# Second block's mixer: row sums from a 65th column of the values that holds 1.0, and distance bias with row maximum as one VectorE operation per map

## The reference, cut to what matters

```
proj = n @ w_in                      # split: c_q c_kv k_r | dq dk dv | mq mk mv
# MLA: 6 heads, causal softmax(q k / sqrt(96)) @ v
# diff: 6 heads with two maps each (width 32), values of width 64
s = q @ k * scale - slope[h] * |pos_q - pos_k|      ; causal mask
p = softmax(s1) - lam * softmax(s2);  o = p @ v
# MoBA: 4 heads of width 64, the same distance bias, one block of 256 keys
s = q @ k * scale - slope[h] * |pos_q - pos_k|      ; causal mask
o = softmax(s) @ v
out = concat(o_mla, rmsnorm(o_diff), o_moba) @ w_out
```

## Time and profile before

| | us |
|---|---|
| time, median of 3 runs (lowest to highest) | 2405.36 (2402.16 to 2407.83) |
| the profiled execution's own time | 2401.76 |
| its span | 2400.0 |
| PE busy in the span | 2357.4 |
| DVE busy | 1726.6 |
| ACT busy | 1446.9 |
| mixer attention, layer 1 of the second stack | from 1575.5 to 1635.4 |
| mixer attention, layer 2 of the second stack | from 2009.3 to 2069.2 |

### The profile page before, as it was taken

How to read it: one execution, slowest core, us unless ns; L and a number is a source line. 1 busy time by engine, 2 the same in 40 slices (tenths; PEclk the granted TensorE clock), 3 DMA queues, 4 the chain that set the end, 5 groups by cost and what they waited for, 6 DMA issues and landing times.

```text
span 2400.0 us, 32057 instructions
## 1 busy us (share of the span) xinstructions
PE 2357.4 (98%) x12122; PEld 1937.0 (81%) x12122; DVE 1726.6 (72%) x2111; ACT 1446.9 (60%) x1761; POOL 69.7 (3%) x79
## 2 busy tenths in 40 slices
PE   9999999999999999999999999999999999999998
PEld 8688888678888888888888888888888888887887
DVE  8664446769898988888989898766465565755555
ACT  6544444657777777777777777564544446554443
POOL 1000000001000000000000000001000000000000
PEclk9999999999999999999999999999999999999999
DMA  7545554429999999999999999516435542452651
GB/s 264 163 158 193 185 186 157 145 82 340 368 345 372 344 377 345 374 339 375 348 369 346 369 350 366 192 54 227 159 124 192 177 145 83 175 187 95 196 190 44
DMA packets 249706, 569.99 MB, mean 237 GB/s; under 512 B 9665, under 2 KB 20353, under 8 KB 249601
## 3 DMA queue, kind: packets, MB, share of 16 engines
q1 hardware_dynamic: 249456, 568.30, 67.1%
q10 hardware_dynamic: 144, 0.26, 0.0%
HBM read 562.82 MB, written 1.05 MB: 235 GB/s over the span
## 4 chain that ended last, share of the span: by engine, by line
PE 92%; DVE 5%; ACT 2%; issue 1%; POOL 0%; POOLq 0%; ACTq 0%; DVEq 0%
PE PS L911 26%; PE PS L913 26%; PE PS L912 26%; PE PS L1064 2%; PE PS L1119 1%; PE PS L1534 1%; PE PS L1076 1%; PE PS L1363 1%; PE PS L1183 1%; PE PS L983 1%; ACT SM L1806 1%; DVE Wl L2216 1%; PE PS L1008 1%; PE PS L1102 1%; PE PS L1324 1%
## 5 line engine op out<-in xcount | busy, mean ns | idle before, releaser
L2645 DVE TENSOR_TENSOR Wl<-ring,Wh 128x2048 fp32r<-128x2048 f32 x334 | 761.6, 2297 | 101.0 <-ACT Wh L1952 101.0
L1952 ACT ACTIVATE Wh<-ring 128x2048 fp32r<-128x2048 f32 x334 | 639.8, 1918 | 127.7 <-PE PS L913 127.7
L2216 DVE TENSOR_TENSOR Wl<-ring,Wh 128x2048 fp32r<-128x2048 f32 (+2 forms) x192 | 431.0, 2251 | 276.6 <-ACT Wh L1713 276.1
L1713 ACT ACTIVATE Wh<-ring 128x2048 fp32r<-128x2048 f32 (+2 forms) x192 | 361.6, 1890 | 235.2 <-PE PS L913 234.2
L911 PE MATMUL PS<-Wh,HTh 128*128 128x512 f32 (+3 forms) x1184 | 464.2, 392 | 4.7 <-DVE Wl L2216 2.4
L913 PE MATMUL PS<-Wh,HTl 128*128 128x512 f32 (+3 forms) x1184 | 456.4, 386 | 0.0
L912 PE MATMUL PS<-Wl,HTh 128*128 128x512 f32 (+3 forms) x1184 | 455.4, 385 | 0.0
L911 PE MATMUL PS<-Wh,xgh 128*128 128x512 f32 x896 | 354.3, 395 | 1.8 <-DVE Wl L2645 1.2
L913 PE MATMUL PS<-Wh,xgl 128*128 128x512 f32 x896 | 349.5, 390 | 0.0
L912 PE MATMUL PS<-Wl,xgh 128*128 128x512 f32 x896 | 348.9, 389 | 0.0
L911 PEld LDWEIGHTS PS<-Wh,HTh 128*128 128x128 f32 x1184 | 222.8, 188 | 50.4 <-issue 4.3
(11 more groups left out here) (349 smaller groups left out, 2422.4 us busy)
## 6 DMA issues: line engine op xcount, KB each, us to landing
ring<-in_moe_w_gate SPq DMA_DIRECT2D x112, 1024.0 KB, 6.9
ring<-in_moe_w_up SPq DMA_DIRECT2D x112, 1024.0 KB, 7.0
ring<-in_moe_w_down SPq DMA_DIRECT2D x112, 1024.0 KB, 6.8
ring<-in_mlp_w SPq DMA_DIRECT2D x64, 1024.0 KB, 5.2
ring<-in_w_in SPq DMA_DIRECT2D x27, 1024.0 KB, 5.3
ring<-in_w_out SPq DMA_DIRECT2D x16, 1024.0 KB, 7.1
ring<-in_cross_wkv SPq DMA_DIRECT2D x16, 1024.0 KB, 12.4
ring<-in_ffn_w_gate SPq DMA_DIRECT2D x14, 1024.0 KB, 5.1
```

The costliest lines, as they stand in the source:

```text
L1713: act.activation(Wh[:, i % SPLITS, 0:n], ring[:, r % RING, 0:n], ACT.Copy).then_inc(w_hi, 1)
L1952: act.activation(Wh[:, (base + i) % SPLITS, :], ring[:, (raw + i) % RING, :], ACT.Copy).then_inc(e_hi, 1)
L2216: dve.tensor_tensor(Wl[:, i % SPLITS, 0:n], ring[:, r % RING, 0:n], Wh[:, i % SPLITS, 0:n].bitcast(F32), ALU.subtract).then_inc(w_lo, 1)
L2645: dve.tensor_tensor(Wl[:, (base + i) % SPLITS, :], ring[:, (raw + i) % RING, :], Wh[:, (base + i) % SPLITS, :].bitcast(F32), ALU.subtract) ...
```

## The change

The values of the three kinds of heads are laid out 65 wide, with the last column set to 1.0 by six `memset`s on DVE at the start of each mixer. The matmul of `values` then gives the row sum of the exponentials as its 65th column, and `end` takes the reciprocal from PSUM. `exps` of these units has no `accum_out`. The bias `dist * s + raw` with its maximum is one `tensor_tensor_reduce` per map that computes (raw + dist) * s and the maximum; for this the queries of the differential and MoBA heads are multiplied with 1/s as they are copied out of PSUM. The columns 1/s are built by POOL at the start, and each copy of two slots with such a factor is now two instructions. Evictions of blocks that hold values are two instructions as well, one of them into the wider layout.

```diff
+                gains = (unsloped(0), unsloped(2, 64)) if slot == 0 else (None, None)
...
+            for k, slopes_ in enumerate(UNSLOPE):
+                pool.memset(unslope[:, k:k + 1], float(np.float32(1.0 / slopes_[0]))).then_inc(pool_seq, 1)
+                n += 1
+            pool.wait_ge(pool_seq, n)
+            for k, slopes_ in enumerate(UNSLOPE):
+                if len(slopes_) > 1:
+                    pool.memset(unslope[64:P, k:k + 1], float(np.float32(1.0 / slopes_[1]))).then_inc(pool_seq, 1)
...
-                            mm = pe.matmul(PS[:, o_bank(un, u), m * dv:(m + 1) * dv],
+                            mm = pe.matmul(PS[:, o_bank(un, u), m * wide:(m + 1) * wide],
...
+                    elif isinstance(gain, list):
+                        for m, g in enumerate(gain):
+                            ins = act.activation(dst[:, m, :], src[:, m, :], ACT.Copy, scale=g)
+                        ins.then_inc(turn_out, 1)
...
-                    if u >= 4:
+                    if u >= 4 and not un["summed"]:
                         act.wait_ge(o_out, u - 3)
                     for m in range(len(un["scores"])):
                         row = SM[:, u % 2, m, 0:un["kl"]]
+                        if un["summed"]:
+                            ins = act.activation(row, row, ACT.Exp, bias=nb[:, u % 2, m:m + 1], scale=un["scale"])
+                            continue
...
+                        src = PS[:, 4 + (c.lin - 1) % 4, :]
+                        if k == 2:
+                            spread_heads(DVS[:, t, 0:4, 0:64], src[:, 256:512], rs_t)
+                            act.activation(proj[:, t, c0:c0 + 256], src[:, 0:256], ACT.Copy, scale=rs_t).then_inc(lin_out, 1)
+                        else:
+                            spread_heads(DVS[:, t, 4:6, 0:64], src[:, 0:128], rs_t)
+                            act.activation(proj[:, t, MQ_AT:MQ_AT + 384], src[:, 128:512], ACT.Copy,
+                                           scale=rs_t).then_inc(lin_out, 1)
...
-                    act.activation(proj[:, t, c0:c0 + n], PS[:, 6, 0:n], ACT.Copy,
-                                   scale=row_rs[:, 0, t:t + 1]).then_inc(lin_out, 1)
+                    rs_t = row_rs[:, 0, t:t + 1]
+                    act.activation(proj[:, t, MK_AT + 128:MK_AT + 256], PS[:, 6, 0:128], ACT.Copy, scale=rs_t)
+                    spread_heads(MVS[:, t, :, 0:64], PS[:, 6, 128:384], rs_t).then_inc(lin_out, 1)
...
-                            ins = dve.scalar_tensor_tensor(out=tile[:, m, :], in0=un["bias"][1], scalar=s,
-                                                           in1=raw[:, m, :], op0=ALU.mult, op1=ALU.add)
+                            ins = dve.tensor_tensor_reduce(tile[:, m, :], raw[:, m, :], un["bias"][1], s, -3e38,
+                                                           ALU.add, ALU.max, mx[:, u % 2, m:m + 1])
                         seq(ins)
-                    if un["bias"] is None or un["bias"][0] != "shared":
+                    if un["bias"] is None:
                         seq(dve.tensor_reduce(mx[:, u % 2, 0:n], tile, AX, ALU.max))
...
-                    seq(dve.reciprocal(cf, sums[:, u % 4, 0:n]))
-                    o = heads_of(PS[:, o_bank(un, u), 0:n * dv], n)
+                    o = heads_of(PS[:, o_bank(un, u), 0:n * un["wide"]], n)
+                    seq(dve.reciprocal(cf, o[:, :, dv] if un["summed"] else sums[:, u % 4, 0:n]))
+                    o = o[:, :, 0:dv]
...
+                for values_ in (DVS, MVS, VV):
+                    for t in range(T):
+                        dve.memset(values_[:, t, :, VW - 1:VW], 1.0)
```

More of the change, by code:

```diff
@@ L80 @@
 SLOPES = [2.0 ** (-8.0 * (h + 1) / (DIFF_H + MOBA_H)) for h in range(DIFF_H + MOBA_H)]
+SLOPE_D = [-SLOPES[h] / DIFF_D ** -0.5 for h in range(DIFF_H)]
+SLOPE_M = [-SLOPES[DIFF_H + h] / 64 ** -0.5 for h in range(MOBA_H)]
+UNSLOPE = [(SLOPE_D[0], SLOPE_D[1]), (SLOPE_D[2], SLOPE_D[3]), (SLOPE_D[4],), (SLOPE_D[5],),
+           (SLOPE_M[0], SLOPE_M[1]), (SLOPE_M[2], SLOPE_M[3])]
 RING = 7
@@ L98 @@
 C2W = 35
+VW = 65
+DV_AT = DV0
+MQ_AT = DV_AT + DIFF_H * VW
+MK_AT = MQ_AT + 256
+MV_AT = MK_AT + 256
+W2 = -(-(MV_AT + MOBA_H * VW) // 16) * 16
 B1W = 4 * HD
@@ L130, in build @@
         proj_at = nc.sbuf_base
-        proj = sb("proj", [P, T, IN2])
+        proj = sb("proj", [P, T, W2])
         scr_at = nc.sbuf_base
@@ L150, in build @@
         mhalf = sb("mhalf", [P, 1])
+        unslope = sb("unslope", [P, 6])
         cols = sb("cols", [P, 2 * C1W + 2 * C2W + EXPERTS * KC])
@@ L204, in build @@
         QN = proj[:, :, 0:MLA_H * NOPE].rearrange("p t (h d) -> p t h d", d=NOPE)
-        VV = scr[:, 22 * S:25 * S].rearrange("p (t h d) -> p t h d", t=T, h=MLA_H)
+        VV = scr[:, 22 * S:22 * S + T * MLA_H * VW].rearrange("p (t h d) -> p t h d", t=T, h=MLA_H)
+        DVS = proj[:, :, DV_AT:DV_AT + DIFF_H * VW].rearrange("p t (h d) -> p t h d", d=VW)
+        MVS = proj[:, :, MV_AT:MV_AT + MOBA_H * VW].rearrange("p t (h d) -> p t h d", d=VW)
         QR = scr[:, 18 * S:21 * S].rearrange("p (t h d) -> p t h d", t=T, h=2 * MLA_H)
@@ L363, in unit @@
             apart = 2 if n == 2 and dv < P else 1
-            return dict(t=t, kl=kl, one=one, scores=scores, bias=bias, scale=scale, values=values, dv=dv, end=end, dst=dst,
+            wide = VW if one and end[0] != "nsa" else dv
+            return dict(t=t, kl=kl, one=one, wide=wide, summed=wide > dv, scores=scores, bias=bias, scale=scale, values=values, dv=dv, end=end, dst=dst,
                         kbs=kbs or [P] * (kl // P), needs=needs, slots=slice(0, n * apart, apart))
@@ L443, in diff_units @@
                             sc.append([(QT[r:r + DIFF_D, slot, tok(t)], QT[r:r + DIFF_D, 4 + slot, 0:kl])])
-                            val.append([proj[:, kb, DV0 + h * 64:DV0 + h * 64 + 64] for kb in range(t + 1)])
-                            slopes.append(-SLOPES[h] / scale)
+                            val.append([DVS[:, kb, h, :] for kb in range(t + 1)])
+                            slopes.append(SLOPE_D[h])
                     dst = heads_of(H[:, t, 384:768], DIFF_H)[:, ha:hb + 1:hb - ha, :]
@@ L458, in moba_units @@
                     sc.append([(QT[r:r + 64, 8 + h // 2, tok(t)], QT[r:r + 64, 10 + h // 2, 0:kl])])
-                    val.append([proj[:, kb, MV0 + h * 64:MV0 + h * 64 + 64] for kb in range(t + 1)])
+                    val.append([MVS[:, kb, h, :] for kb in range(t + 1)])
                 scale = 64 ** -0.5
-                bias = ("slopes", dist[:, t, 0:kl], [-SLOPES[DIFF_H + h] / scale for h in order])
+                bias = ("slopes", dist[:, t, 0:kl], [SLOPE_M[h] for h in order])
                 dst = H[:, t, 768:1024].rearrange("p (b a d) -> p a b d", a=2, b=2)
@@ L508, in build, with chunks_batch, unsloped @@
         cross_extras = {0: t_cross_q[2:4]}
-        def chunks_batch(chunks, slot, rows=P):
-            return ([c for chunk in chunks for c in chunk], QT[0:rows, slot:slot + len(chunks), :], None)
+        def chunks_batch(chunks, slot, rows=P, gain=None):
+            return ([c for chunk in chunks for c in chunk], QT[0:rows, slot:slot + len(chunks), :], gain)
+        def unsloped(k, rows=P):
+            return [unslope[0:rows, k + m:k + m + 1] for m in range(2)]
         def plain_chunk(src, c0, n=P):
@@ L521, in build @@
         for c0, slot in ((DQ0, 0), (DK0, 4)):
[L522 to L525, removed]
+            gains = (unsloped(0), unsloped(2, 64)) if slot == 0 else (None, None)
+            t_diff.append(chunks_batch([plain_chunk(proj, c0), plain_chunk(proj, c0 + P)], slot, gain=gains[0]))
+            t_diff.append(chunks_batch([plain_chunk(proj, c0 + 256, 64), plain_chunk(proj, c0 + 320, 64)], slot + 2, 64,
+                                       gains[1]))
+        t_moba = [chunks_batch([plain_chunk(proj, c0 + P * b) for b in range(2)], slot, gain=unsloped(4) if slot == 8 else None)
+                  for c0, slot in ((MQ_AT, 8), (MK_AT, 10))]
         qn, kn = ([plain_chunk(src, P * b) for b in range(3)] for src in (proj, H))
@@ L1115, in values @@
                         pe.wait_ge(o_out, u - 1)
[L1116 removed]
+                    wide = un["wide"]
                     for m, vs in enumerate(un["values"]):
                         for kb, v in enumerate(vs):
[L1119 removed]
+                            mm = pe.matmul(PS[:, o_bank(un, u), m * wide:(m + 1) * wide],
                                            PT[0:un["kbs"][kb], u % 2, kb, m, :], v,
@@ L1821, in copies @@
                     before_x = sum(len(extras.get(k, ())) for k in range(i))
-                    for x, (srcs, dst, _) in zip(extra[before_x:], extras.get(i, ())):
+                    for x, (srcs, dst, gain) in zip(extra[before_x:], extras.get(i, ())):
                         act.wait_ge(pt_full, x + 1)
                         cols_ = sum(s.shape[0] for s in srcs)
-                        act.activation(dst, PS[0:dst.shape[0], 4 + x % 2, 0:cols_].rearrange(
```

(27 more changed lines are left out.)

1 line of the change is left out of this document (added).

## The result

| | before | after |
|---|---|---|
| time, median (lowest to highest, runs) | 2406.24 us (2402.16 to 2407.83, 4) | 2430.95 us (2430.64 to 2433.84, 4) |
| profiled execution's own time, span | 2401.76, 2400.0 us | 2430.98, 2429.2 us |
| mean granted clock of the profiled execution | 0.998 | 0.996 |

The ratio is 1.0096, with a 95% interval from 1.0079 to 1.0114: slower by 24.7 us, where 1.9 us less was forecast. The forecast of 2403.5 us and its range up to 2407.0 were wrong.

What follows compares the result with a forecast made beforehand. PE was taken as the bound, with DVE and ACT edits paying only where PE waits; -1.9 us of closed gaps plus 0.1 took the median from 2405.4 to 2403.5 us, range 2400.5 to 2407.0.

Steps and rivals of the forecast that it cites:

- the sum: Whole kernel: -1.9 us from both mixers' gaps plus 0.1 for wider values, taken as -1.9 to -1.8 us.
- Rest: Reciprocal from PSUM 0 to 0.1 us a mixer; DVE's memsets covered by slack, POOL's fills free.
- The bound: PE sets the time; its idle time in both mixer attentions, 3.8 us in all, limits the gain.
- Unit 1: Mixer transposes after `last_block`, waiting for ACT: shorter exponentials recover 0.41 us in the first mixer, 0.44 in the second.
- It just holds: Second key block's transposes wait for the MoBA queries' copy, ending near 1586.3 us; PE gets there at 1586.43.
- Unit 5: Mixer transposes after `unread`: ACT's row ends 0.51 us earlier where 0.52 was lost; gain about 0.5 us each.
- The accumulator's read: ACT's exponentials in the mixers: dropping the sum saves 0.09 us a map, 0.37 us a unit.
- Rival C: ACT gets longer: the read costs nothing, added copies remain, 0.53 us a mixer; 2406.5 us, chance 0.08.
- Rivals B and E: B: gaps reopen at next PE-ACT round trip, 2405.4 us, chance 0.14. E: all mixer idle goes, 2400.1 us, chance 0.08.
- Bias and maximum: DVE in the mixers: about 7 us a mixer go, hidden, since PE did not wait for it.
- The 65th column: PE's values products, 132 records a mixer: at most 0.16 us more by the trace, 0.1 taken.
- rival D: Values products of 65 columns last as long as 256, costing 31 us; 2436 us, chance 0.03.

Runs made afterwards that it cites:

- run 1: Kernel before with nothing but 128 unused bytes per partition ahead of `scr`; 2436.79 us, ratio 1.0109.
- run 2: Changed kernel with rows of `proj` 2368 wide instead of 2352, so `scr` lies 256 bytes later than before the change; 2409.22 us, ratio 0.9990.
- Run 5: Changed kernel with rows of `proj` 2368 wide, values multiplied 64 wide and sums left with the exponentials; 2405.11 us, one execution.
- run 6: Changed kernel with rows of `proj` 2368 wide, sums from the 65th column, mask as before and queries unscaled; 2407.24 us, one execution.
- run 10: Kernel before with 256 unused bytes ahead of `scr`; 2407.53 us, ratio 0.9999.
- run 3: Kernel before with 128 unused bytes ahead of `Wh`, so everything behind `ring` lies 128 bytes later; 2412.03 us.

## Why the prediction was wrong

**The step that failed** is the sum: -1.9 + 0.1. It has a term for every instruction that the change adds, drops or moves, and none for the size of `proj`. The part *Rest* lists the memsets and POOL's fills and calls them free; that the wider values push all later tensors by 128 bytes isn't costed anywhere. That term is +27.0 us: 5136 products that the diff doesn't touch, 5 ns each. Runs 1 and 2 show it from both sides. The prediction's own sign of being wrong, a window outside the mixers that changes by more than 0.3 us, is what the next profile showed. No rival covered it: in each of them the change could only act through its own instructions.

**The bound.** That PE sets the time, and that edits on DVE and ACT pay only where PE waits, held. What was drawn from it, that at most 3.8 us can move, didn't follow: it limits what waits can give, and says nothing of the pace of products that already run without a wait.

**Unit 1.** Forecast 0.41 in the first mixer and 0.44 in the second. Measured at the transposes: 0.42 and 0.39. "It just holds" was true in the first mixer only. In the second, unit 1's second key block starts 0.63 us after its first, in place of 0.46, and 0.22 us of the gain is lost again within two records. Timeline of the second mixer:

```profile
2047.69 0.82 ACT L1866 ACTIVATE scr<-PS,unslope 128x256 f32<-128x256 f32 x2
...
2047.94 1.29 PE L1105 MATMUL PS<-ident,SM 128*128 128x128 f32 x8
```

The MoBA queries' copy, now two instructions of 0.82 us together, ends at 2048.51, and the transposes of the second block start at 2048.57. Run 5 loses the same 0.22 us there in both mixers, and run 6, without the second instruction, in neither: this is the cost of the split copy.

**Unit 5.** Forecast about 0.5 in each, of 0.52 and 0.51 lost; measured 0.47 and 0.47. The transposes start 0.85 us behind `unread`, not 0.80.

**What was missed in the mixers.** Unit 4's transposes gained 0.11 to 0.12 us, a wait hidden in their modelled length (four of them last 0.66 us in run 5, and 0.60 us in the earlier trace rows where nothing waits). In the second mixer unit 0's gained 0.29. Together the first mixer has 0.42 + 0.11 + 0.47 = 1.0 of the 1.11 found, the second 0.29 + 0.39 - 0.22 + 0.12 + 0.47 = 1.05 of 1.09; smaller steps make the rest.

**The accumulator's read.** 0.09 us a map was taken, from the earlier trace rows. With it, exponentials of 128 and 256 columns started 0.385 and 0.49 us apart; without it, 0.292 and 0.40 (medians), so 0.093 us a map was right. Rival C, for which the read had to cost under 0.03, falls with this and with the gain at unit 5. An exponential of 256 columns lasts 502 ns in the new kernel, so it overlaps the next by 0.10 us. For this overlap the Trainium skill ("ScalarE: Activation LUTs", What ACT_TABLE_LOAD costs) gives about 93 ns; the trace agrees.

**Rivals B and E.** Neither came: the gain at units 1 and 5 is still there at the mixer's end, and at 1.1 us a mixer it is far from the 2.65 that E needed.

**Bias and maximum at no gain.** Right (run 5), with 418 ns a map where 421 was taken. The added copies cost 0.33 us a mixer where nothing else hides them.

**The 65th column.** 0.1 us was taken, 0.16 at most; none was found, the step being 1.90 us in both kernels. So rival D is wrong, though its 2436 lies near the result: it had a dearer values step, and that didn't change. A number that comes out near says nothing for its mechanism. The Trainium skill ("TensorE: Matmul & The Clock Gate", Back-to-back issue gap) puts a floor under 64 columns that a 65th leaves; no run here shows a difference. The prediction's estimate from that page, a cycle or so a pass, was worked out wrongly: the page's formula for the warm array, N / 2.4 + 2.5 ns, gives 29.6 ns for 65 columns against a floor of about 25, an estimate of 4.6 ns a pass.

**What stays open.** That the distance of the two operands modulo 256 bytes sets the pace is shown for 512-column products of these tensors; why it does is not. Whether the loading of weights, the streaming, or their order in the memory is what collides, no trace here tells; the records of these weight loads have a median of 188 ns in both kernels. Nor is it settled why at 192 bytes one product of three keeps its pace. Distances other than 0, 32, 64, 96, 128 and 192 weren't tried. Records of other shapes show nothing clear: the 128-column transposes stay at a median of 109 ns before, after, and in all ten runs.

## What to carry to other kernels

A change of a tensor's size is a change of the address of every tensor declared behind it. Where PE is the bound, as here, first work out by how much the streamed operands and the weights shift against each other, and keep these distances (here multiples of 256 bytes) with unused columns; this costs nothing (run 10) and was worth 27 us. When a time moves by more than the edited stage's idle time allows, compare the starts of records that the edit doesn't touch, ahead of the edited stage first. And test such a suspicion on the old kernel with padding alone, since this separates the place from the code in one run.

## What the runs showed of the hardware

The pace of back-to-back 512-column products depends on where their two operands lie: 227 ns from start to start at a distance moved by 0 or 256 bytes, 231 or 232 at 128, 232 to 235 at 32, 64 and 96, and 226 to 232, by product, at 192. Shifting both operands alike by 128 bytes changes nothing (run 3). The Trainium skill ("TensorE: Matmul & The Clock Gate", Step-by-step: what each phase is for) says that loading the next weights takes no read bandwidth from the running matmul; the runs show 2.3% fewer products in 1000 us of the experts, and this hangs on the relative address of just these two operands, so they are not independent of each other here. What makes it is not shown. The loss repeats: the experts last 1074.2 us in run 1 and in the changed kernel alike.
